# The context rows' second normalisation moved into the output projection, and the memory rows turned last

## The reference, cut to what matters

```
# last layer of the first block (only the 1024 token rows are kept)
x = layer_norm(ALPHA * x + gate * (mixed @ w_out), ln_g, ln_b)        # 1024 x 1024
# second block
h_res = layer_norm(x, ln_in_g, ln_in_b)                               # 1024 x 1024
mem_n = layer_norm(mem, mem_ln_g, mem_ln_b)                           # 256 x 1024
for l in range(2):
    proj = h_res @ w_in[l]                                            # 1024 x 3236
    mkv  = mem_n @ w_mem_kv[l]                                        # 256 x 512
    ... attention of four kinds, gated ...
    h_res = layer_norm(ALPHA * h_res + mixed @ w_out[l], ln_g[l], ln_b[l])
```

## Time and profile before

| what | value |
|---|---|
| runs | 4544.51, 4553.86, 4561.49 us; median 4553.86 |
| the profiled execution, its own time | 4551.49 us |
| its span, first to last instruction | 4549.7 us |
| mean granted TensorE clock | 0.939 of 2.4 GHz |
| TensorE matmul busy | 3941.9 us (87%) |
| VectorE busy | 2703.4 us (59%) |
| GpSimd busy | 1564.4 us (34%) |
| ScalarE busy | 1532.3 us (34%) |

### The profile page before, as it was taken

One profiled execution on the slowest core, in us unless ns is written; L12 is line 12 of the kernel. 1 busy time (PEld: TensorE's weight loads), 2 busy tenths in 40 slices (PEclk: granted clock), 3 DMA queues, 4 the chain that ended last, 5 costly groups with the idle time before them and its releaser, 6 DMA issues. The chain is left out here.

```text
span 4549.7 us, 105346 instructions
## 1 busy us (share of the span) xinstructions
PE 3941.9 (87%) x44016; PEld 3086.2 (68%) x44016; DVE 2703.4 (59%) x4530; ACT 1532.3 (34%) x2727; POOL 1564.4 (34%) x1256
## 2 busy tenths in 40 slices
PE   5999888877998699979886998689878988987898
PEld 4878678854676587758884666568735667873566
DVE  3456445555666536645555666675576766557676
ACT  1233223333552123323232554210145621014562
POOL 2233144412014423314441211665332255533225
PEclk8999999988999799989998999889989999998999
DMA  5545533343146455562334134533412464341236
GB/s 191 162 171 185 171 97 82 84 180 84 43 109 186 139 150 200 186 188 70 83 86 158 44 84 139 183 105 111 141 58 62 102 184 133 110 142 56 62 99 186
DMA packets 566726, 569.47 MB, mean 125 GB/s; under 512 B 150472, under 2 KB 464476, under 8 KB 564244
## 3 DMA queue, kind: packets, MB, share of 16 engines
q1 hardware_dynamic: 438740, 485.33, 35.1%
q10 hardware_dynamic: 127616, 78.95, 6.1%
HBM read 375.92 MB, written 192.42 MB: 125 GB/s over the span
## 5 line engine op out<-in xcount | busy, mean ns | idle before, releaser
L1096 PE MATMUL pr_acc<-hH,pr_wh 128*128 128x512 f32 (+1 forms) x1288 | 481.5, 374 | 0.0
L1097 PE MATMUL pr_acc<-hL,pr_wh 128*128 128x512 f32 (+1 forms) x1288 | 465.4, 361 | 0.0
L1098 PE MATMUL pr_acc<-hH,pr_wl 128*128 128x512 f32 (+1 forms) x1288 | 465.2, 361 | 0.0
L2755 ACT ACTIVATE an_p<-an_p,an_stat 128x1280 f32<-128x1280 f32 (+5 forms) x372 | 339.7, 915 | 133.4 <-DVE an_stat L2812 129.8
L2708 PE MATMUL an_t<-ident,an_p 128*128 128x128 f32 x2152 | 312.9, 281 | 36.2 <-ACT an_pT L2762 23.5
L2487 POOL TENSOR_TENSOR an_kl<-mo_w,an_kh 128x1280 fp32r<-128x1280 f32 (+3 forms) x36 | 79.3, 2203 | 751.3 <-DVE an_qh L2477 751.2
L2808 DVE CUSTOM_DVE_ANT_0 an_p<-an_s,an_mask 128x256 f32<-128x256 f32 (+8 forms) x308 | 275.1, 893 | 96.6 <-PE an_s L2691 63.3
L1465 POOL TENSOR_TENSOR sp_sl<-sp_w,sp_sh 128x512 fp32r<-128x512 f32 x172 | 245.9, 1437 | 197.4 <-DVE sp_sh L1540 178.9
L2708 PEld LDWEIGHTS an_t<-ident,an_p 128*128 128x128 f32 x2152 | 236.7, 141 | 110.1 <-ACT an_pT L2762 46.2
L2004 DVE TENSOR_TENSOR rk_tu<-rk_tu,rk_ps 128x512 f32<-128x512 f32 x300 | 189.1, 683 | 195.1 <-PE rk_ps L1828 194.9
L1140 POOL TENSOR_TENSOR pr_wl<-pr_w,pr_wh 128x1024 fp32r<-128x1024 f32 x58 | 143.3, 2471 | 467.1 <-DVE pr_wh L1160 467.1
(11 more groups left out here) (380 smaller groups left out, 9716.8 us busy)
## 6 DMA issues: line engine op xcount, KB each, us to landing
CHK<-ri_out SPq DMA_DIRECT2D x24, 1920.0 KB, 8.0
rk_in<-CHK SPq DMA_DIRECT2D x240, 128.0 KB, 2.5
pr_w<-in_w_in ACTq DMA_DIRECT2D x58, 512.0 KB, 4.4
UT<-pr_out SPq DMA_DIRECT2D x45, 640.0 KB, 4.5
sp_w<-in_w_in ACTq DMA_DIRECT2D x50, 512.0 KB, 5.2
U<-sp_c SPq DMA_DIRECT2D x100, 256.0 KB, 2.0
mod_w<-in_w_mod SPq DMA_DIRECT2D x16, 1024.0 KB, 7.9
mo_w<-in_w_out SPq DMA_DIRECT2D x16, 1024.0 KB, 6.0
```

The costliest lines, as they stand in the source:

```text
L1096: nc.tensor.matmul(out, wh[:, u, k, 0:m], hi, start=(k == 0), stop=False)
L1097: nc.tensor.matmul(out, wh[:, u, k, 0:m], lo, start=False, stop=False)
L1098: ins = nc.tensor.matmul(out, wl[:, u, k, 0:m], hi, start=False, stop=(k == KT - 1))
L2755: nc.scalar.activation(row, row, ACT.Exp, bias=stat[:, n % NPM, j, 1:2], scale=heads[groups[n][0]].scale, accum_out=total[:, sum_column(n, ...
```

## The change

`mixed_out` takes a further argument, `again`, two vectors (offset and gain) of a second normalisation. It is given in the first block's last layer alone. Each block of rows then passes statistics, power, norm, scale and shift a second time before it is stored, one step behind the first: in step t, VectorE does summed(t), stats_again(t - 1), gated(t + 3), scaled(t), scaled_again(t - 1), and the other engines likewise. `XB` then holds what `HA` held; `HA` goes. In `second_projection` only the two memory blocks are normalised, in layer 0; token blocks come first in the order, memory blocks last, with nine buffers in place of six; SP loads four token blocks, the first memory block, the vectors and four more token blocks without a wait, and the second memory block once the first buffer is free. The last four of the 32 units are those of memory.

```diff
@@ second_projection
-    NX, NT, R, NP = 6, 4, 8, (N2 + 2 * P - 1) // (2 * P)
+    NT, R, NP = 4, 8, (N2 + 2 * P - 1) // (2 * P)
...
-    rows = [T["mem" if first else "MEMN"][b * P:(b + 1) * P, :] for b in range(MB)] + [src[b * P:(b + 1) * P, :] for b in toks]
-    NB = len(rows)
-    normed = list(range(NB)) if first else []
-    vectors = [[T["ln_in_b"], T["ln_in_g"]], [T["mem_ln_b"], T["mem_ln_g"]]] * first
+    M0, NB = len(toks), len(toks) + MB
+    rows = [src[b * P:(b + 1) * P, :] for b in toks] + [T["mem" if first else "MEMN"][b * P:(b + 1) * P, :] for b in range(MB)]
+    normed = [M0, M0 + 1] if first else []
+    vectors = [T["mem_ln_b"], T["mem_ln_g"]]
...
-    units = [("mem", b, h) for b in range(MB) for h in range(2)]
-    upto = [2, 4]
+    units, upto = [], []
     for j in range(NT):
         units += [(B11, j, None), (B21, j, None)]
         upto.append(len(units))
         units += [(B22, j, None), (T1, j, None), (T3, j, None), (T2, j, None), (T4, j, None)]
+        upto.append(len(units))
+    for b in range(MB):
+        units += [("mem", b, h) for h in range(2)]
         upto.append(len(units))
...
-            x = core.sb(s1, "sp_x", [P, NX, DM])
+            x = core.sb(s1, "sp_x", [P, NB - 1, DM])
@@ second_projection, SP
-                for t in range(NX, NB):
-                    b = t - NX
-                    if b in keeps:
-                        keep(b)
-                    sp.wait_ge(turned.sem, turned.nth(upto[b] if b < MB else upto[b - b % 2] + 1))
...
-                    if b in keeps:
-                        sp.wait_ge(kept.sem, kept.after(keeps.index(b) + 1))
-                    load(t)
-                for t in keeps[NB - NX:]:
-                    keep(t)
+                for t in range(4):
+                    load(t)
+                for t in range(M0, NB - 1):
+                    load(t)
+                if first:
+                    for q, row in enumerate(vectors):
+                        sp.dma_start(v[:, q, :], row.to_broadcast([P, DM])).then_inc(v_in.sem, 16)
+                for t in range(4, M0):
+                    load(t)
+                sp.wait_ge(turned.sem, turned.nth(upto[0] + 1))
+                sp.wait_ge(t_pool.sem, t_pool.nth(3))
+                sp.wait_ge(t_dve.sem, t_dve.nth(1))
+                load(NB - 1)
+                for i, t in enumerate(normed):
+                    sp.wait_ge(z_ok.sem, z_ok.nth(i + 1))
+                    sp.dma_start(T["MEMN"][i * P:(i + 1) * P, :], xs(t)).then_inc(kept.sem, 16)
@@ second_projection, ScalarE, GpSimd, VectorE
-                    centre(t + 3)
+                    centre(t + 6)
...
+                for t in range(NB):
+                    power(t + 6)
+                    shift(t + 4)
+                    if t < M0 and t % 2:
+                        j = t // 2
...
-                    stats(t + 3)
-                    scale(t + 2)
-                    if t >= 3 and t % 2:
-                        j = (t - 3) // 2
+                    stats(t + 6)
+                    scale(t + 5)
+                    if t < M0 and t % 2:
+                        j = t // 2
@@ mixed_out, ScalarE
+                def norm_again(t):
+                    act.wait_ge(nb2.sem, nb2.nth(2 * t + 2))
+                    zz, small = z[:, t % NZ, :], sm[:, t % 2, 16:32]
+                    nc.scalar.activation(zz, zz, ACT.Identity, bias=small[:, 15:16], scale=small[:, 14:15]).then_inc(nrm2.sem, 1)
...
                     norm(t)
+                    if again and t:
+                        if t > 1:
+                            store(t - 2)
+                        norm_again(t - 1)
                     if t + NY < nblk:
                         upper(t + NY)
-                    if t:
+                    if t and not again:
                         store(t - 1)
-                store(nblk - 1)
+                if again:
+                    norm_again(last)
+                    store(last - 1)
+                store(last)
@@ mixed_out, GpSimd
+                def power_again(t):
+                    small = sm[:, t % 2, 16:32]
+                    pool.wait_ge(st2.sem, st2.nth(t + 1))
+                    nc.gpsimd.tensor_tensor(small[:, 14:15], small[:, 13:14], core.minus_half[:], ALU.pow).then_inc(nb2.sem, 1)
+                    pool.wait_ge(nb2.sem, nb2.nth(2 * t + 1))
+                    nc.gpsimd.tensor_tensor(small[:, 15:16], small[:, 12:13], small[:, 14:15], ALU.mult).then_inc(nb2.sem, 1)
+
+                def shift_again(t):
+                    pool.wait_ge(sc2.sem, sc2.nth(t + 1))
+                    zz = z[:, t % NZ, :]
+                    nc.gpsimd.tensor_tensor(zz, zz, vecs[:, len(vectors) - 2, :], ALU.add).then_inc(fin2.sem, 1)
...
                     power(t)
+                    if again and t:
+                        power_again(t - 1)
                     if t + NY < nblk:
                         lower(t + NY)
                     if t + 1 < nblk:
                         shift(t)
+                    if again and t:
+                        shift_again(t - 1)
+                if again:
+                    power_again(last)
@@ mixed_out, VectorE
+                def stats_again(t):
+                    zz, small = z[:, t % NZ, :], sm[:, t % 2, 16:32]
+                    c = Chain(chain2, t, 2)
+                    dve.wait_ge(fin.sem, fin.nth(t + 1))
+                    for h in range(2):
+                        ins = V.bn_stats(small[:, h * 6:(h + 1) * 6], zz[:, h * 512:(h + 1) * 512])
...
+                def scaled_again(t):
+                    zz = z[:, t % NZ, :]
+                    dve.wait_ge(nrm2.sem, nrm2.nth(t + 1))
+                    V.tensor_tensor(zz, zz, vecs[:, len(vectors) - 1, :], ALU.mult).then_inc(sc2.sem, 1)
+                    if t == last:
+                        dve.wait_ge(sc2.sem, sc2.nth(t + 1))
+                        V.tensor_tensor(zz, zz, vecs[:, len(vectors) - 2, :], ALU.add).then_inc(fin2.sem, 1)
...
                 for t in range(nblk):
                     summed(t)
+                    if again and t:
+                        stats_again(t - 1)
                     if t + NY < nblk:
                         gated(t + NY)
                     scaled(t)
+                    if again and t:
+                        scaled_again(t - 1)
+                if again:
+                    stats_again(last)
+                    scaled_again(last)
@@ block_one
-                      lambda tok: xs[at(tok, P), :], lambda tok: xo[at(tok, P), :], T["UT"])
+                      lambda tok: xs[at(tok, P), :], lambda tok: xo[at(tok, P), :], T["UT"], [T["ln_in_b"], T["ln_in_g"]] if last else None)
@@ block_two
-        src, dst = (T["HA"], T["HB"]) if l == 0 else (T["HB"], out)
-        second_projection(core, l, x if l == 0 else src)
+        src, dst = (x, T["HB"]) if l == 0 else (T["HB"], out)
+        second_projection(core, l, src)
```

More of the change, by code:

```diff
@@ L1404, in centre @@
                         act.wait_ge(st.sem, st.nth(i + 1))
-                        nc.scalar.activation(xs(t), xs(t), ACT.Identity, bias=sm[:, t, 15:16]).then_inc(less.sem, 1)
-                for t in range(3):
-                    centre(t)
+                        nc.scalar.activation(xs(t), xs(t), ACT.Identity, bias=sm[:, i, 15:16]).then_inc(less.sem, 1)
                 u = 0
@@ L1474, in stats @@
                     i = normed.index(t)
+                    small = sm[:, i, :]
                     c = Chain(chain, i, 2)
@@ L1590, in second_projection @@
     nn = len(normed)
-    spent([(c, 1) for c in x_in + v_in] + [(kept, len(keeps)), (m_stored, 4), (st, nn), (pw, nn), (less, nn), (chain, 2 * nn),
+    spent([(c, 1) for c in x_in] + [(v_in, int(first)), (kept, len(normed)), (m_stored, 4), (st, nn), (pw, nn), (less, nn), (chain, 2 * nn),
           (scaled, nn), (z_ok, nn), (t_pool, 3 * NT), (t_dve, NT), (turned, NU), (up, NU), (low, NU), (m_out, 4), (w_in, NP + 2), (stored, NP),
@@ L2854, in win_rows, with mixed_out @@
     return first - win_row(b), first - r + 7
-def mixed_out(core, weights, toks, ncm, ready, gates, ln, scales, x_src, dst, utd):
+def mixed_out(core, weights, toks, ncm, ready, gates, ln, scales, x_src, dst, utd, again=None):
     nc, T = core.nc, core.t
@@ L2865, in mixed_out @@
     gate = scales is not None
-    vectors = ln + (scales[0] if gate else [])
+    vectors = ln + (scales[0] if gate else []) + (again or [])
     nt = NK - ncm
```

90 lines of the change are left out of this document (39 added, 51 removed).

## The result

| | kernel before | changed kernel |
|---|---|---|
| median of 12 runs of each, us | 4557.26 (4544.51 to 4561.49) | 4568.07 (4556.79 to 4578.57) |
| ratio, 95% interval | | 1.0021 (1.0011 to 1.0030) |
| profiled execution: time, span, mean granted clock | 4551.49, 4549.7, 0.939 | 4556.79, 4555.0, 0.939 |
| output projection: 2800.8 to the second projection's first SP issue | 118.2 | 147.2 |
| opening, layer 0: first SP issue to first weight product | 76.3 | 53.8 |

What follows compares the result with a forecast made beforehand. The GpSimd and ScalarE chain was taken to bound the output projection, not TensorE. Output projection +27.8, layer 0's opening -19.4, layer 1's -0.7 gave +7.7 us: forecast 4561 us, range 4543 to 4578.

Steps and rivals of the forecast that it cites:

- The period: Output projection loop: GpSimd and ScalarE's closed chain grows from 11.24 to 14.74 us; +11.65 over blocks 1 to 4.
- rival A: Output projection: TensorE's products set the old period and hide the loop's additions; net -4.0 us, 4550; chance 0.13.
- The vectors: Start of the output projection: two added vectors' loads delay ScalarE's third tanh; +2.8 us, bounds 0 and 3.
- The upper bound of the lock: Output projection loop: six added shifts each wait for VectorE's two-input sum, 6.2 us more; the short shift was taken.
- The tail: End of the output projection, after the gating: second normalisation of blocks 5, 6 and the last uncovered; +13.3 us.
- Block 5: Output projection's tail: waits for the last shift_again (2.35) and scaled_again (1.22); +3.6 us.
- the last part: Output projection behind the last block: the second normalisation runs serially with nothing to cover it; +8.3 us.
- block 6: Output projection's tail: scaled_again at 1.22 and a small wait; +1.4 us.
- The opening of layer 0: Second projection's start: last memory block lands at 24.4, then a 32.5 us chain; 56.9 from 76.3, -19.4 us.
- The opening of layer 1: Second projection, layer 1: VectorE's first difference moves into ScalarE's 5.21 us stall; -0.7 us, bounds 0 and -3.
- B: Layer 0's opening is limited by data alone, 45.0 us instead of 56.9; net -4.2, 4550; chance 0.15.
- C: Output projection: idle gaps drop TensorE's clock, products run at 1.2 GHz; net +25.5 us, 4579; chance 0.10.

Runs made afterwards that it cites:

- e9: Changed kernel with VectorE's second multiplication by gamma cut to 8 of 1024 columns, except in the last block: one run 4544.06 us, output projection 143.4.
- e3: Changed kernel with ScalarE issuing its second pair of weight halves four steps later: one run 4552.89 us, openings 52.1 and 38.95.
- e2: Kernel before with the second normalisation added to the output projection, old second projection kept: one run 4584.85 us, layer 1's opening 40.4.
- e11: The kernel of e10 again, timed in five rounds: median 4547.72 us, ratio to the kernel before 0.9988 (0.9975 to 1.0001).
- e10: Changed kernel with the second projection's old order: memory rows first, six buffers, only memory blocks normalised: one run 4544.63 us, openings 42.8 and 38.6.
- e6: Changed kernel with ScalarE's second normalisation behind the upper halves instead of ahead: one run 4563.97 us, output projection 149.9.

## Why the prediction was right, point by point

- **The period.** The chain was read right: 14.74 forecast, 14.66 to 14.75 measured; e9 rules out that VectorE's amount of work sets it (the 1.0 us for which the shift waits for VectorE's sum stays in), and sums that wait for no product exclude TensorE (rival A, periods of 11 to 12). Only the first period is smaller than said, 11.24 + 0.63 and not + 1.15. The last lower starts 13.4 us later than in the kernel before (2900.42 against 2887.05), where 2.8 + 11.65 = 14.5 were forecast.
- **The vectors.** +2.42 at the third tanh, against +2.8.
- **The upper bound of the lock.** Under load shift_again takes 2.40, as when it meets nothing: the short value was right in the loop. The Trainium skill (SBUF — State Buffer, Who interferes with whom) says that the order of issue decides who waits, for the whole instruction. The trace agrees in both directions: VectorE begins 0.11 us behind GpSimd and takes 3.31 instead of 1.22; in the same interval GpSimd's shift_again takes 3.33 at 2915.21, behind VectorE's two-input sum (2914.20 to 2916.35).
- **The tail.** Block 5 +3.6 (3.6 forecast), the last part +8.3 (+8.3), block 6 +3.5 where I said 1.4. That term was mis-sized: I counted scaled_again at its free 1.22 "and a small wait", and it cost 3.31. From the start of VectorE's scale (2920.63) to the next sum (2925.28) pass 4.65 us where 1.14 passed before, which is the whole +3.5. The shift_again of 3.33 in the same interval cost nothing here: GpSimd's power behind it starts 5.6 us after the sum, as before (5.5).
- **The opening of layer 0.** 53.8 against 56.9. The mechanism (the landing of the last memory block, then power and shift ahead of the row sums) is in the rows, both halves 1.5 us shorter than counted: 22.9 and 30.9 against 24.4 and 32.5. What I had not seen is that VectorE would be late by ScalarE's stall, so that the landing and the stall compete for the same place; e3 shows them to be interchangeable.
- **The opening of layer 1.** This step failed in sign: -0.7 forecast, +2.1 measured. I kept the stall at 5.21 us though the change issues nine loads in one row ahead of it instead of six; it grew to 7.88. The step of the prediction that failed is this term, held constant. The old code's 40.4 and 40.9 in e2 and e11 do not make it scatter, as the granted clock shows. The third of four pairs of blocks turned, in e10 (38.6 us) and e11 (40.9), one and the same code:

```profile
3771.36:3776.41 5.05, 3.79 (x29) 2.99 (x29) 4.88 (x9) 3.81 (x7) 4.27 (x4) 1.00 0.01 3
...
3764.48:3770.55 6.07, 4.94 (x28) 4.70 (x28) 5.26 (x9) 3.91 (x7) 3.27 (x3) 0.72 0.00 0
```

In before and e10 the clock is at 1.00 from this pair on, in e2 and e11 it falls once more, and this pair and the one before it take 13.64 us together instead of 11.33. That is 2.3 us, the whole difference between e11 and e10. In the eight profiles of the new order with the stall (40.3 to 40.8) the clock stays at 1.00 there. At the same clock the new order so costs 1.5 to 2.2 us in layer 1.
- **Rivals.** A is excluded by the period, though more narrowly than I wrote: a product takes 11.1 us (48 matmuls, busy 11.13 us from 2903 to 2915), not 10.5, beside an old period of 11.24. B is excluded by 53.8 instead of 45. C is excluded by the time, not by the clock alone. TensorE stood idle 1.42, 3.52 and 1.92 us ahead of the products of blocks 5, 6 and 7. Behind the 3.52 us the clock fell: that product began at 2888.35, ran eight matmuls 0.43 us apart and then went on at 0.23. It ended at 2901.1, and the sum that needs it stands at 2912.95. The other two products ran at 1.00 throughout. The rule that the Trainium skill gives in TensorE: Matmul & The Clock Gate (HAM oscillation), by which C would happen, acted once in this loop, for one group and not for every group, and cost nothing.

Open: why the clock falls a second time in layer 1's opening in two profiles of the old order and not in the two others. The rest of the execution behind that opening took 755.0 us in the changed kernel and 759.3 in the one before, and the stretch between the two openings 757.4 against 756.3, which is why the two profiles differ by 5.3 us and not by 8.6. It is no gain: old code in e10 and e11 took 755.7 and 751.4, and over all profiles both codes cover 751 to 759.

## What to carry to other kernels

Work that is moved into another stage is paid there at the rate of that stage's closed chain: here three periods of 11.2 us grew by 3.4 to 3.5 each and the serial end by 15.4, though every engine had idle time. Before moving rows that need work to the end of a load queue, count the chain behind the last landing; the rows with the longest chain go first (e10 against the change, 11 us). And taking one link out of such a chain is worth little if it shifts the start of VectorE's two-input instructions behind GpSimd's: e6 took out 1.13 us and got 1.0 back.

## What the runs showed of the hardware

- An issue of one weight load by ScalarE took 6.62 and 7.88 us in the changed kernel (6.6 to 8.4 over both layers of all profiles with nine loads ahead of it), 3.7 to 5.2 in layer 1 of the old order, and 0.4 to 1.1 otherwise (e3: 1.01 for two). ScalarE's next copy started within 0.1 us of the end of that issue, having stood idle for 6.43 and 7.71 us.
- A two-input instruction of VectorE of 1.22 us took 2.4 to 3.3 when GpSimd's 2.4 us instruction had begun 0.1 to 1.1 us before it, and GpSimd's 2.35 took 3.3 in the opposite case.
- In the openings the turning of one pair of blocks took 7.1 us at a granted clock of 0.76 and 5.05 at 1.00. In e3 the clock was lower where TensorE had waited 2.0 to 2.2 us for each pair; in the changed kernel it was higher behind the work that had piled up. There a stall of 7.9 us cost 1.9.
- The granted clock was 1.00 in a stretch in which TensorE did nothing but turn rows: in e10 from 3771.36 to 3776.41, busy 3.79 of 5.05 us. The same code ran at 0.72 in e11.
